# Decode value products in a hybrid decoder step: four pages per interruption of the weight products instead of two

## The chip, the cores and the metric

The kernel runs on one core of a Trainium2 chip. The metric is the device time of one execution in microseconds (us), as the median of several runs. TensorE does the matrix products, VectorE (DVE), ScalarE (ACT) and GpSimd (POOL) the rest; SyncE (SP) issues most of the DMAs.

## What is computed

One step of a decoder layer with two parallel groups, for a prompt of 512 tokens and for 8 sequences that each decode one token against 2048 cached positions (16 pages of 128 positions):

```
z = rms_norm(x) @ w_in                       # q | k | v | forget logits | lru x | lru gate
att: softmax(q.k/sqrt(d) + forget bias) @ v  # 8 heads of 128; decode rows read paged keys and values
lru: causal conv -> RG-LRU -> gelu(gate) * h # 8 blocks of 128 channels
x = x + concat(rms_norm(att), rms_norm(lru)) @ w_out
x = x + relu(rms_norm(x) @ w_up)^2 @ w_down
```

The change concerns the decode part of `softmax(...) @ v`: for each of the 8 sequences the probabilities of 2048 cached positions times the cached values, page by page. One value page is 128 positions x 8 heads x 128, 512 KB.

## The kernel before

The 520 token columns (512 of the prompt, 8 decoded) stay in on-chip memory, split into a high and a low part, `XH` and `XL`. The input weights come in units of 128 columns (1 MB each, two DMAs into `RAW`); ScalarE copies a unit into its high part `WH` (L743, `split_hi`), VectorE subtracts to get the low part `WL` (L1213, `split_lo`), and TensorE does 16 x 6 products of 128x260 per unit (L1896 and L1900). There are two slots of each buffer.

The middle of the kernel is eight steps, i = 0 to 7, one per attention head, per recurrent block and per decode sequence at once. A step has four units, q = 0 to 3, and TensorE's order in it is written out by hand: a unit has 32 half-steps n, and `insert` names what is done behind half-step n. "(q, n)" below is such a place. In step i stand:

- the value products of sequence i-1 (`VALUES_AT`) and the rest of those of sequence i-2 (`OLDER_AT`): eight interruptions of two pages each. They are the calls of TensorE's `values`, which multiply one column of probabilities (`PP`) by a page in `VR`, at L2057. Each page, once done, releases its slot (`v_used`);
- `queries` at (0,13), `max_rows` at (0,15), `max_all` at (0,25) (L2160), `head_scores` at (1,5) (L2084 to L2086), `transpose_probs` at (2,7) (L2095), `attend` at (2,19) (L2105), `rows` at (3,7), and the recurrent gates (L2247) at the end.

VectorE's order is written out too. Behind `max_all` it subtracts the maximum (`shift`, L1422 and L1423), finishes the recurrence, copies the query (`next_query`, L1499), scores key pages 0 to 3 (L1349 and L1351), splits a weight unit (L1213), takes the row maxima of the prompt's scores (L1506), scores pages 4 and 5, and scales the probabilities (`normalized`, L1517); `transpose_probs` waits for those. Then follow further key pages, the convolution (L1403 to L1408), a split, and the last key pages.

Value pages go through a ring of `NVS` = 4 slots in `VR`, key pages through another of 4 in `KR`. SyncE issues, in order, the value pages (L524) and the weight units (L439); before it asks for a page it waits until the page four earlier is used. GpSimd issues the key pages from a queue of its own. After step 7 come the output units (`out_unit`), in which the last pages of sequence 6 and all of sequence 7 are done, and then the feed-forward part.

Of the kernel before, what the change touches and what calls it, by code (L numbers as in the profile page):

```python
# [19 lines left out]
def hymba_step(nc, x_prompt, x_sample, cache_k, cache_v, cache_logf, state_conv, state_h, page_table,  # L20
# [14 lines left out]
    NB = x_sample.shape[0]  # L35
# [4 lines left out]
    NH, HD = cache_k.shape[3], cache_k.shape[4]  # L40
    DA = NH * HD
    NL = (D - DA) // P
    NPG = page_table.shape[1]
# [7 lines left out]
    NKS, NVS = 4, 4  # L51
# [45 lines left out]
    with ExitStack() as ctx:  # L97
# [214 lines left out]
        def at(n, half):  # L312

            return n % 2, n // 2 + half
# [11 lines left out]
        def one(i):  # L326
            return bass.ds(i, 1)
# [81 lines left out]
        PT_BANK = [(4, 0), (5, 0), (6, 0), (6, 256)]  # L409
        PT_AT = [0, 512, 896, 1152]  # L410

        VALUES_AT = {(1, 21): 0, (2, 5): 2, (2, 21): 4, (3, 5): 6, (3, 21): 8}
        OLDER_AT = {(0, 5): 10, (0, 21): 12, (1, 3): 14}
        MT_PS, MAX_PS = PS[0:NH, 6, P:2 * P], PS[:, 6, 2 * P:2 * P + NH]
        MT_LAST, MAX_LAST = PS[0:NH, 4, 3 * P:4 * P], PS[:, 5, 3 * P:3 * P + NH]
        VO = PS[:, 7, 0:2 * HD]
# [8 lines left out]
        def _(sp):  # L425
            def load_unit(n, half, src, peeled=False):
                slot, w = at(n, half)
                if not peeled:

                    sp.wait_ge(lo_done, 2 * w + slot - 1)  # L430
                for part in range(2):
                    load_part(slot, src, part)
# [8 lines left out]
            def cols(view, c):  # L441
                return view[:, :, bass.ds(c, P)]
# [6 lines left out]
            for j in range(TT):  # L449
                sp.dma_start(XT[:, j, :], x_prompt[0, j * P:(j + 1) * P, :]).then_inc(x_in[j], 16)  # L450
                for src, r in rows[3 * j:3 * j + 3]:
                    n = src.shape[0] * src.shape[1] // P
# [30 lines left out]
            def out_cols(u):  # L483

                rows = slice(NH, KD) if u < CH else slice(0, NH)
                c = P * out_tile(u % CH, 0)
                return w_out_v[:, rows, c:c + 2 * P]

            def step(i, head, prev, nxt, older=True):
                def values(h, pages):  # L490
                    for b in pages:
                        value_page(h, b, not older)

                for q in range(4):
                    if q == 0 and prev and older:
                        values(i - 2, range(12, 14))
                    if q and prev:
                        values(i - 1, range(4 * q - 4, 4 * q - 2))
                    if head:
                        src = [lambda: cols(w_in_v, COL_X + P * i), lambda: cols(w_in_v, COL_G + P * i),  # L500
                               lambda: cols(w_in_v, DA + P * (i + 1)) if nxt else out_cols(0),
                               lambda: cols(w_in_v, 2 * DA + P * (i + 1)) if nxt else out_cols(1)][q]()
                        load_unit(U_L + 2 + q, 2 * i, src)
                    else:
                        load_unit(U_O + 2 + q, 0, out_cols(2 + q))
                    if head and q == 1:
                        if prev:
                            sp.wait_ge(gates_ps, i)
                        sp.dma_start(GW[:, 0, :], w_gate_a[0, one(i), :, :].rearrange("a p c -> p (a c)")).then_inc(gw_full, 16)
                        sp.dma_start(GW[:, 1, :], w_gate_x[0, one(i), :, :].rearrange("a p c -> p (a c)")).then_inc(gw_full, 16)  # L510
                    if q == 0 and prev and older:
                        values(i - 2, range(14, NPG))
                    if q and prev:
                        values(i - 1, range(4 * q - 2, 4 * q))
                if not head:
                    load_unit(U_O + 6, 0, out_cols(6))
                    values(i - 1, range(12, NPG))

            def value_page(h, b, first):

                g = page(h, b)
                if not first or b >= NVS:
                    sp.wait_ge(v_used, NPG * h + b - NVS + 1)
                sp.dma_start(VR[:, b % NVS, :], v_pages[one(g), :, :].rearrange("a p f -> p (a f)"))\  # L524
                  .then_inc(v_full[b % NVS], 16)
# [1358 lines left out]
        def _(pe):  # L1884
# [51 lines left out]
            def out_unit(u, insert={}):  # L1936

                slot, w = at(U_O + u, 0)
                k0 = NH if u < CH else 0
                pe.wait_ge(lo_done, 2 * w + slot + 1)  # L1940
                for m in range(2):
                    out_products(u, m, range(k0, k0 + NH), {n - 2 * NH * m: f for n, f in insert.items()})
# [23 lines left out]
            for j in range(TT):  # L1966
                pe.wait_ge(x_in[j], 16)
                for c in range(4):
                    if j:
                        pe.wait_ge(x_ready[1], 4 * (j - 1) + c + 1)  # L1970
                    for n in range(4):
                        k = 4 * c + n
# [42 lines left out]
            for j in range(TT - 1):  # L2015
                n = TT - 1 - j
# [25 lines left out]

            unit(U_L - 1, 0, U_L - 1, 0, {17: [first_rows]})

            def values(h, b0):

                if b0 == 0:
                    pe.wait_ge(pp_ready, h + 1)
                    if isinstance(h, int) and h == 0:
                        pe.wait_ge(vo_clear, 1)  # L2050
                    else:
                        pe.wait_ge(pvs_ready, h)
                for b in (b0, b0 + 1):
                    pe.wait_ge(v_full[b % NVS], 16 * (NPG // NVS * h + b // NVS + 1))
                    for n in range(NH):
                        half, m = n // NHH, n % NHH
                        ins = mm(PS[VQ * m:VQ * m + 1, 7, half * HD:(half + 1) * HD], PP[:, n, b:b + 1],  # L2057
                                 VR[:, b % NVS, n * HD:(n + 1) * HD], start=b == 0 and half == 0, stop=b == NPG - 1,
                                 skip_group_check=True)
                    ins.then_inc(v_used, 1)  # L2060
# [28 lines left out]
            def transpose_probs(h):  # L2089

                pe.wait_ge(p_norm, h + 1)
                for j in range(TT):
                    bank, c = PT_BANK[j]
                    for t in range(j, TT):
                        ins = tr(PS[:, bank, c + (t - j) * P:c + (t - j + 1) * P],  # L2095
                                 PR[:, P_AT[t] + j * P:P_AT[t] + (j + 1) * P], ident[:, :])
                    if j != 2:
                        ins.then_inc(pt_ps, 1)

            def attend(h):  # L2100

                pe.wait_ge(vtok_ready, h + 1)
                for j in range(TT):
                    pe.wait_ge(pt_ready, 3 * h + min(j + 1, 3))
                    ins = mm(PS[:, 4, j * P:SEQ], vtok[:, j, :], PT[:, PT_AT[j]:PT_AT[j] + (TT - j) * P],  # L2105
                             start=j == 0, stop=j == TT - 1)
                ins.then_inc(att_ps, 1)
# [44 lines left out]
            def max_rows(i, dst=MT_PS):  # L2152

                pe.wait_ge(m8_ready, i)
                tr(dst, M8[:, :], ident[:, :]).then_inc(mt_ps, 1)

            def max_all(i, dst=MAX_PS):

                pe.wait_ge(md_ready, i)
                mm(dst, ones[0:NH, :], MD[:, :], start=True, stop=True).then_inc(max_ps, 1)  # L2160

            def step(i, head, prev, older=True, final=False):
# [54 lines left out]
                def places(q, n):  # L2217

                    f = []
                    if prev and (q, n) in VALUES_AT:  # L2220
                        f.append(lambda: values(i - 1, VALUES_AT[q, n]))
                    if prev and older and (q, n) in OLDER_AT:
                        f.append(lambda: values(i - 2, OLDER_AT[q, n]))
                    if (q, n) in extra:
                        f.append(extra[q, n])
                    return f
# [32 lines left out]
            h, last_b = NH - 1, NB - 1  # L2259
            slot, w = at(U_O, 0)  # L2260
            pe.wait_ge(lo_done, 2 * w + slot + 1)
            for k in range(NH, KD):
                for m in range(2):
                    out_products(0, m, [k], ready={0: (xl_ready, KD + k - NH + 1)})
                if k == NH + 1:
                    values(last_b - 1, 10)
                if k == NH + 4:
                    values(last_b - 1, 12)

            def head_scores():  # L2270
                pe.wait_ge(shifted, NB)
                scores(h, last=True)
                value_cols(last_b - 1)

            out_unit(1, {3: [lambda: values(last_b - 1, 14)], 7: [lambda: max_rows(NB, MT_LAST)], 11: [lambda: max_all(NB, MAX_LAST)],
                         14: [head_scores]})
            out_unit(2, {7: [lambda: transpose_probs(h)], 13: [lambda: values(last_b, 0)], 19: [lambda: attend(h)],
                         27: [lambda: values(last_b, 2)]})
            out_unit(3, {3: [lambda: values(last_b, 4)], 11: [lambda: values(last_b, 6)], 19: [lambda: values(last_b, 8)],
                         27: [lambda: values(last_b, 10)]})  # L2280
            out_unit(4, {3: [lambda: values(last_b, 12)], 11: [lambda: values(last_b, 14)], 17: [last_states], 23: [merge_sums]})
            out_unit(5, {5: [lambda: value_cols(last_b)], 13: [lru_sums]})
            out_unit(6, {3: [att_sums]})
            out_unit(7, {13: [sample_rows]})
# [188 lines left out]
```

## Time and profile before

| | |
|---|---|
| median of 3 runs | 2301.18 us (2300.08 to 2302.46) |
| span of the profiled execution | 2298.8 us |
| TensorE matmul busy | 2255.5 us, 98% |
| VectorE busy | 1605.5 us, 70% |
| ScalarE busy | 858.9 us, 37% |
| DMA over the span | 160 GB/s |
| value products (L2057) | 2048 records, 67.8 us busy |

The profile gives the busy time of each engine, groups of instructions by source line, who waited for whom, and the chain of work that ended last, followed back from the last instruction. Matmuls are pipelined, so the distance between two starts tells more than the length of one. A row of the timeline gives the start, the length of the run of like instructions, engine, line, operation, operands, how many, and in square brackets the idle time before it with what ended it. An fp32 product shows as two records.

### The profile page before, as it was taken

How to read it: one execution, taken by the hardware profiler on the slowest of the kernel's cores; microseconds unless marked ns; L12 is line 12 of the kernel's file. 1: busy time of each engine (PE TensorE's matmuls, PEld its weight loads, DVE VectorE, ACT ScalarE, POOL GpSimd, SP SyncE). 2: the span in 40 equal slices, each digit the busy share in tenths (PEclk: the TensorE clock that was granted, in tenths of full speed). 3: DMA queues.
4: the chain of work that ended last, by engine and by line, in shares of the span. 5: the costliest groups of instructions: out<-in, count | busy, mean ns of one | idle time of the engine just before them, and what ended most of it. 6: DMA issues, size and time to landing. Idle time of an engine off the chain costs nothing.

```text
span 2298.8 us, 50026 instructions
## 1 busy us (share of the span) xinstructions
PE 2255.5 (98%) x19889; PEld 2196.1 (96%) x19889; DVE 1605.5 (70%) x2043; ACT 858.9 (37%) x1201; POOL 154.0 (7%) x194
## 2 busy tenths in 40 slices
PE   7999999999999999999999999999999999999997
PEld 6999898989988999999999999999999999999997
DVE  7349889988884597876576576576576576576563
ACT  5124433344454233343243243243243243243245
POOL 0001111111114031000000000000000000000002
PEclk8999999999999999999999999999999999999998
DMA  7458999999985333333433433433433433433422
GB/s 239 106 159 261 323 330 327 317 314 327 317 290 191 98 127 84 114 96 99 138 93 98 137 93 98 137 93 99 137 94 98 137 93 99 137 93 99 137 89 97
DMA packets 386972, 368.47 MB, mean 160 GB/s; under 512 B 12259, under 2 KB 350596, under 8 KB 385844
## 3 DMA queue, kind: packets, MB, share of 16 engines
q1 hardware_dynamic: 359828, 295.38, 41.9%
q0 software_dynamic: 18608, 67.64, 8.2%
q10 hardware_dynamic: 8448, 4.20, 0.6%
q8 instruction: 65, 1.06, 0.2%
q14 instruction: 23, 0.19, 0.0%
HBM read 354.22 MB, written 12.94 MB: 160 GB/s over the span
## 4 chain that ended last, share of the span: by engine, by line
PE 87%; DVE 6%; DVEq 2%; issue 2%; ACT 1%; DMA 1%; SPq 1%; ACTq 0%
PE PS L1896 37%; PE PS L1900 18%; PE PS L2344 9%; PE PS L2343 9%; PE PS L2342 9%; DVE KR L1349 2%; PE PS L2057 2%; DVEq L1507 1%; PE PS L2105 1%; DVE WL L1213 1%; PE PS L2247 1%; DVE SC L1351 0%; ACT WH L743 0%; PE PS L2095 0%; DVE NM L1506 0%
## 5 line engine op out<-in xcount | busy, mean ns | idle before, releaser
L1093 ACT ACTIVATE WH<-RAW 128x1024 fp32r<-128x1024 f32 x293 | 304.9, 1056 | 679.8 <-PE PS L1900 521.5
L1647 DVE TENSOR_TENSOR WL<-RAW,WH 128x1024 fp32r<-128x1024 f32 x293 | 358.3, 1223 | 133.8 <-ACT WH L1093 132.4
L1896 PE MATMUL PS<-XH,WH 128*128 128x260 f32 x1952 | 408.6, 291 | 10.4 <-DVE XL L1278 6.2
L1896 PE MATMUL PS<-HH,WH 128*128 128x260 f32 x2048 | 412.5, 282 | 1.4 <-DVE HL L1652 0.7
L1900 PE MATMUL PS<-HH,WL 128*128 128x260 f32 x2048 | 411.7, 282 | 0.0
L1896 PE MATMUL PS<-HL,WH 128*128 128x260 f32 x2048 | 410.8, 282 | 0.0
L1896 PE MATMUL PS<-XL,WH 128*128 128x260 f32 x1952 | 393.7, 283 | 0.0
L1900 PE MATMUL PS<-XH,WL 128*128 128x260 f32 x1952 | 393.3, 283 | 0.0
L1750 DVE TENSOR_TENSOR A<-A,PS 128x520 f32<-128x520 f32 x256 | 177.5, 696 | 264.5 <-PE PS L1900 263.8
L1896 PEld LDWEIGHTS PS<-XH,WH 128*128 128x128 f32 x1952 | 301.4, 189 | 28.3 <-issue 19.5
L1896 PEld LDWEIGHTS PS<-HH,WH 128*128 128x128 f32 x2048 | 314.6, 188 | 2.1 <-issue 1.1
L1896 PEld LDWEIGHTS PS<-HL,WH 128*128 128x128 f32 x2048 | 316.1, 188 | 0.0
L1900 PEld LDWEIGHTS PS<-HH,WL 128*128 128x128 f32 x2048 | 315.4, 188 | 0.0
L1900 PEld LDWEIGHTS PS<-XH,WL 128*128 128x128 f32 x1952 | 302.3, 189 | 0.0
L1896 PEld LDWEIGHTS PS<-XL,WH 128*128 128x128 f32 x1952 | 302.1, 189 | 0.0
L2342 PE MATMUL PS<-XH,WH 128*128 128x260 f32 x960 | 271.6, 283 | 0.0
L2344 PE MATMUL PS<-XH,WL 128*128 128x260 f32 x960 | 271.0, 282 | 0.0
L2343 PE MATMUL PS<-XL,WH 128*128 128x260 f32 x960 | 270.9, 282 | 0.0
L1213 DVE TENSOR_TENSOR WL<-RAW,WH 128x2048 fp32r<-128x2048 f32 x61 | 139.6, 2288 | 105.2 <-ACT WH L743 105.1
L2343 PE MATMUL PS<-TX,WH 128*128 128x260 f32 x720 | 203.4, 283 | 0.0
L2344 PE MATMUL PS<-TX,WL 128*128 128x260 f32 x720 | 203.3, 282 | 0.0
L2342 PE MATMUL PS<-TX,WH 128*128 128x260 f32 x720 | 202.4, 281 | 0.0
(335 smaller groups left out, 3085.6 us busy)
## 6 DMA issues: line engine op xcount, KB each, us to landing
KR<-in_cache_k POOLq DMA_DIRECT2D x128, 512.0 KB, 6.0
VR<-in_cache_v SPq DMA_DIRECT2D x128, 512.0 KB, 6.3
RAW<-in_w_up SPq DMA_DIRECT2D x128, 512.0 KB, 4.2
RAW<-in_w_down SPq DMA_DIRECT2D x128, 512.0 KB, 4.5
RAW<-in_w_in SPq DMA_DIRECT2D x82, 512.0 KB, 6.6
RAW<-in_w_out SPq DMA_DIRECT2D x32, 512.0 KB, 5.5
TMP<-in_w_up SPq DMA_DIRECT2D x30, 512.0 KB, 6.1
xT_spill<-A SPq DMA_DIRECT2D x1, 4160.0 KB, 16.3
```

The lines of the kernel that those rows point to most:

```text
L1093: nc.scalar.activation(RING_H[SLOT[i]], RB[b], ACT.Copy).then_inc(f_hi, 1)
L1213: V.tensor_tensor(WL[slot][:, :], RAW[:, slot, :], WH[slot][:, :].bitcast(F32), ALU.subtract)\
L1349: V.tensor_tensor(KR[:, b % NKS, :], KR[:, b % NKS, :], QB[:, :], ALU.mult).then_inc(dve_prod, 1)
L1507: dve.drain()
L1647: V.tensor_tensor(RING_L[SLOT[i]], RB[op_block(i)], RING_H[SLOT[i]].bitcast(F32), ALU.subtract).then_inc(f_lo, 1)
L1750: V.tensor_tensor(rows, rows, pair_view(pair), ALU.add).then_inc(d_out[pair // 2], 1)
L1896: mm(dsts[c], wh(k), x[:, k, c * HT:(c + 1) * HT], start=first and n == 0 and x is xh, stop=False)
L1900: ins = mm(dsts[c], wl(k), xh[:, k, c * HT:(c + 1) * HT], start=False, stop=last and n == len(kts) - 1)
L2057: ins = mm(PS[VQ * m:VQ * m + 1, 7, half * HD:(half + 1) * HD], PP[:, n, b:b + 1], VR[:, b % NVS, n * HD:(n + 1) * HD], start=b == 0 and h ...
L2342: mm(dst, wh[:, w], xh[:, k, :], start=q < 3 and k == 0, stop=False, skip_group_check=True)
L2343: mm(dst, wh[:, w], xl[:, k, :], start=False, stop=False, skip_group_check=True)
L2344: ins = mm(dst, wl[:, w], xh[:, k, :], start=False, stop=q in (3, 5, 6) and k == KB - 1, skip_group_check=True)
```

## The change

The value products of a sequence are taken four pages at a time instead of two. In step i the places are now (1,21), (2,21) and (3,21) for pages 0 to 3, 4 to 7 and 8 to 11 of sequence i-1, and (0,21) for pages 12 to 15 of sequence i-2. The places (2,5), (3,5), (0,5) and (1,3) are no longer used. SyncE asks for the four pages of a unit ahead of the unit's weights, where it asked for two ahead of them and two behind. In output unit 0 the call for pages 10 and 11 of sequence 6 is dropped, since they are now done in step 7; the calls behind it, all of sequence 7 among them, keep their two pages.

```diff
-        VALUES_AT = {(1, 21): 0, (2, 5): 2, (2, 21): 4, (3, 5): 6, (3, 21): 8}
-        OLDER_AT = {(0, 5): 10, (0, 21): 12, (1, 3): 14}
+        VALUES_AT = {(1, 21): 0, (2, 21): 4, (3, 21): 8}
+        OLDER_AT = {(0, 21): 12}
...
+                ahead = 4 if head else 2
                 for q in range(4):
                     if q == 0 and prev and older:
-                        values(i - 2, range(12, 14))
+                        values(i - 2, range(12, 12 + ahead))
                     if q and prev:
-                        values(i - 1, range(4 * q - 4, 4 * q - 2))
+                        values(i - 1, range(4 * q - 4, 4 * q - 4 + ahead))
...
                     if q == 0 and prev and older:
-                        values(i - 2, range(14, NPG))
+                        values(i - 2, range(12 + ahead, NPG))
                     if q and prev:
-                        values(i - 1, range(4 * q - 2, 4 * q))
+                        values(i - 1, range(4 * q - 4 + ahead, 4 * q))
...
-            def values(h, b0):
+            def values(h, b0, pages):
...
-                for b in (b0, b0 + 1):
+                for b in range(b0, b0 + pages):
...
-                        f.append(lambda: values(i - 1, VALUES_AT[q, n]))
+                        f.append(lambda: values(i - 1, VALUES_AT[q, n], NVS))
                     if prev and older and (q, n) in OLDER_AT:
-                        f.append(lambda: values(i - 2, OLDER_AT[q, n]))
+                        f.append(lambda: values(i - 2, OLDER_AT[q, n], NVS))
...
-                if k == NH + 1:
-                    values(last_b - 1, 10)
                 if k == NH + 4:
-                    values(last_b - 1, 12)
+                    values(last_b - 1, 12, 2)
```

## Rows read from the trace of the kernel before

**Rows 1.** The page: span, and busy time of TensorE's matmuls and weight loads

```profile
span 2298.8 us, 50026 instructions
...
PE 2255.5 (98%) x19889; PEld 2196.1 (96%) x19889; DVE 1605.5 (70%) x2043; ACT 858.9 (37%) x1201; POOL 154.0 (7%) x194
```

**Rows 2.** Windows: one head step, busy us of each engine, granted clock, DMA share

```profile
core 0: us, PE busy (x) PEld busy (x) DVE busy (x) ACT busy (x) POOL busy (x), PEclk, DMA share, GB/s
...
477.90:545.10 67.20, 66.76 (x702) 60.53 (x701) 60.48 (x78) 26.98 (x44) 8.45 (x16) 1.00 0.95 322
```

**Rows 3.** TensorE's timeline round one interruption, and all value products by line

```profile
499.24 0.40 PE L1900 MATMUL PS<-XH,WL 128*128 128x260 f32 x2
499.57 1.05 PE L2057 MATMUL PS<-VR,PP 128*1 128x128 f32 x32
500.56 0.51 PE L1896 MATMUL PS<-XH,WH 128*128 128x260 f32 x2
500.90 0.41 PE L1896 MATMUL PS<-XL,WH 128*128 128x260 f32 x2
...
L2057 PE MATMUL PS<-VR,PP 128*1 128x128 f32 x2048 | 67.8, 272 | 2.2 <-DMA VR<-in_cache_v 2.2
```

**Rows 4.** The chain that ended last, same step: start us, us, what

```profile
478.20 0.61 DVEq L1375
...
488.97 1.22 DVE KR L1349
...
500.66 1.29 DVE PR L1517 x4
501.99 1.31 PE PS L2095 x10
...
510.49 0.98 PE PS L2057 x32
```

**Rows 5.** TensorE's timeline, same step, only the inserted work

```profile
483.12 0.38 PE L2084 MATMUL PS<-kT,qcur 128*128 128x128 f32 x2
...
501.99 1.20 PE L2095 MATMUL PS<-ident_r,PR 128*128 128x128 f32 x9 [0.44 <-DVE PR L1517]
...
510.42 1.05 PE L2057 MATMUL PS<-VR,PP 128*1 128x128 f32 x32
...
525.16 1.05 PE L2057 MATMUL PS<-VR,PP 128*1 128x128 f32 x32
...
529.84 1.88 PE L2247 MATMUL PS<-XC,GW 128*128 128x512 f32 x4
```

**Rows 6.** VectorE's timeline, same step

```profile
477.84 0.17 DVE L1422 COPY MX<-PS 128x8 f32 x1 [1.27 <-PE PS L2160]
...
481.48 0.41 DVE L1499 COPY qcur<-A 128x512 f32 x1
...
500.66 1.27 DVE L1517 TENSOR_SCALAR PR<-PR,RSUM 128x128 f32<-128x128 f32 x4
...
527.73 0.19 DVE L1408 COPY CVALL<-XW 128x24 f32 x1
```

**Rows 7.** TensorE's waits, 196 to 760 us: total us, times, longest

```profile
PE PS L2095 <- DVE PR L1517: 3.8, 6, 1.6
...
PE PS L2155 <- DVE M L1493: 1.6, 1, 1.6
```

**Rows 8.** The chain that ended last, from step 7's gates on

```profile
665.69 0.36 PE PS L2249 x4
...
667.65 1.81 ACT WH L743
...
687.26 0.30 DVE M L1493
687.60 0.29 PE PS L2155
```

**Rows 9.** SyncE's page requests; page landings in 511:525 (step 5), 242:257, 578:592

```profile
511.24 1.50 SPq L524 DMA_DIRECT2D VR<-in_cache_v  x2
...
DMA to landing us min/median/max: 5.0/7.5/9.2
...
DMA to landing us min/median/max: 5.5/9.8/12.6
...
DMA to landing us min/median/max: 7.3/10.0/13.7
```

**Rows 10.** Weight requests in 580:586 with their landings, and the split that reads them

```profile
L439 SPq DMA_DIRECT2D RAW<-in_w_in x2: 384/467/550, 581.0 to 581.6; - x2
...
DMA to landing us min/median/max: 7.8/11.4/15.0
...
600.75 1.93 ACT L743 ACTIVATE WH<-RAW 128x2048 fp32r<-128x2048 f32 x1
```

More of the change, by code:

```diff
@@ L2273, in head_scores @@
                 value_cols(last_b - 1)
-            out_unit(1, {3: [lambda: values(last_b - 1, 14)], 7: [lambda: max_rows(NB, MT_LAST)], 11: [lambda: max_all(NB, MAX_LAST)],
+            out_unit(1, {3: [lambda: values(last_b - 1, 14, 2)], 7: [lambda: max_rows(NB, MT_LAST)], 11: [lambda: max_all(NB, MAX_LAST)],
                          14: [head_scores]})
[L2277 to L2281, printed above, removed]
+            out_unit(2, {7: [lambda: transpose_probs(h)], 13: [lambda: values(last_b, 0, 2)], 19: [lambda: attend(h)],
+                         27: [lambda: values(last_b, 2, 2)]})
+            out_unit(3, {3: [lambda: values(last_b, 4, 2)], 11: [lambda: values(last_b, 6, 2)], 19: [lambda: values(last_b, 8, 2)],
+                         27: [lambda: values(last_b, 10, 2)]})
+            out_unit(4, {3: [lambda: values(last_b, 12, 2)], 11: [lambda: values(last_b, 14, 2)], 17: [last_states], 23: [merge_sums]})
             out_unit(5, {5: [lambda: value_cols(last_b)], 13: [lru_sums]})
```

## The prediction

> **What bounds the kernel now.** I read first the profile's first part, then the windows of one head step, then the chain that ended last. TensorE is busy 98% of the span [rows 1], so the change, which takes work from TensorE, looks like pure gain. The windows warn: in a head step (67.2 us) TensorE is busy 66.76 us, VectorE 60.48 us and the DMA engines 0.95 of the time [rows 2]. Three resources are nearly full, and which ends last must be read place by place. The clock is granted in full there (1.00 in the same row, the 2.4 GHz level), so no term here changes with it.
>
> The chain of waits answers it [rows 4]. In each head step it leaves TensorE when the cross-head maximum is done (`max_all`, half-step (0,25)), runs through VectorE alone, and comes back to TensorE at `transpose_probs`, half-step (2,7), where TensorE had stood idle 0.44 us for the scaled probabilities [rows 5]. VectorE begins that stretch having waited 1.27 us for TensorE, at 477.84, and ends it at 501.93 (500.66 + 1.27): 24.1 us in which it waits for nothing of note [rows 6]. From (2,7) round to the next (0,25) the chain is TensorE's own. So one period is the sum of two parts: 24.1 us of VectorE plus the handovers, then TensorE from (2,7) to (0,25). TensorE's work from (0,25) to (2,7) is no part of the sum; it is 0.44 us shorter than VectorE's.
>
> **What an interruption costs.** The value products of two pages are 32 records in 1.05 us [rows 3]. They run four at a time: eight fours, each record 0.27 us long, so a four follows the last after (1.05 − 0.27)/7 = 0.11 us, and a page, four fours, is 0.44 us. The weight products start a pair every 0.24 us. Round an interruption the starts go 499.24, then 500.56 and 500.90; undisturbed the last of them would be at 499.72. The interruption therefore takes 1.18 us, of which 0.88 is pages and 0.30 is switching in and out. A page costs the same wherever it stands; only the 0.30 can be saved.
>
> **What the change removes.** All value products are 2048 records, so 64 interruptions of 32 [rows 3]. After the change heads 0 to 5 take four each (24), head 6 takes three of four pages and two of two (5), head 7 keeps its eight: 37. Gone are 27, worth 27 × 0.30 = 8.1 us of TensorE's time. No trace row shows a group of 64 records. From one side, its second half could cost nothing extra; from the other, it could run slower than 0.11 us per four. The nearest row is the uniform group of 32, so I take 0.44 us a page, with no surcharge.
>
> **Where the work lands.** Now the two parts separately.
> - (0,25) to (2,7): the groups at (1,3) and (2,5) go, the one at (1,21) doubles. TensorE saves 2 × 1.18 − 0.88 = 1.48 us here. VectorE's 24.1 us are untouched (the change doesn't edit it, and its start hangs on (0,25)), so TensorE arrives earlier and waits longer: 0.44 + 1.48 = 1.92 us at `transpose_probs`. Worth to the period: nothing. At (1,5) `head_scores` loses its 1.23 us of slack as well (VectorE's query copy ends at 481.89, TensorE comes at 483.12 [rows 5, 6]); a tenth of a us of wait there would be inside the same cover.
> - (2,7) to (0,25): the groups at (3,5) and (0,5) go, those at (2,21), (3,21) and (0,21) double. Before: 5 groups with 10 pages. After: 3 groups with 12 pages, because pages 14 and 15 came across from (1,3). That is 2 × 0.44 − 2 × 0.30 = +0.28 us, on the path, each step.
>
> So a change that saves TensorE time makes the period longer. Six such sections lie between the (2,7) of steps 1 to 6 and the (0,25) of steps 2 to 7: +1.7 us. The cover exists in each: the wait at `transpose_probs` is there in steps 1 to 6, six times, 3.8 us in all, 1.6 us the longest (step 1, which only gets longer) [rows 7]; step 7 has a wait near zero, so there at most 0.05 us is gained.
>
> The last step: from its (2,7) to its gate products the groups at (2,21) and (3,21) double and (3,5) goes, 0.88 − 0.30 = +0.58 us. From the gates the chain is ScalarE's and VectorE's up to `max_rows` [rows 8], where TensorE stands idle 1.6 us [rows 7]. The removed group of pages 10 and 11 in output unit 0 is under that idle time: it becomes 1.6 + 1.18 us of waiting, and the end is 0.58 us later. Behind that nothing is changed; head 7 keeps its pairs, and its waits for pages hang on TensorE's own release of slots.
>
> The wait of VectorE for `max_all` covers small slips: from the gates to (0,25) TensorE gets 1.18 − 0.88 = 0.30 us shorter, leaving 1.27 − 0.30 = 0.97 us.
>
> **What SyncE's queue does.** Its four requests are made at the same point as its first two were: each waits for the slot of four pages earlier, free only when the products at the (q,21) before are done. Two requests take 1.50 us from the first's start to the second's end, so they follow each other at about 1.17 us. The fourth is out about 0.83 + 3 × 1.17 = 4.3 us after the group starts at 510.42 [rows 5, 9]. Queued behind them are the unit's two weight requests, moved back by 2 × 1.17 = 2.3 us and behind 1 MB more, and at q = 1 the gate weights. ScalarE's split waits for these weights. In the slowest case a weight part took 15.0 us to land (asked 581.6, landed 596.6) and the split began at 600.75 [rows 10]: 4.1 us of slack, which 1 MB at 320 GB/s [rows 2] cuts by 3.3 us. With the 0.97 us above I take zero here; its upper bound is a few tenths of a us in one step. Key requests are in GpSimd's queue and are not moved; VectorE's page scores behind (2,7) have 2 us of cover up to the gate products (convolution done at 527.92, gates at 529.84 [rows 5, 6]), plus the new 0.58.
>
> **Sum.** 6 × 0.28 + 0.58 = 2.3 us. The profiled span is 2298.8 us, the median of the runs 2301.18, so 2.4 us lie around the span. I forecast a span of 2301.1 and a time of 2303.4 us: +0.10%, no change that a measurement of this kernel tells from zero (it takes about 0.2%, 4.6 us: 2296.6 to 2305.8). The 0.30 is the softest number: with 0.42 the sum is 1.2 us, with 0.20 it is 3.6, so 2302.4 to 2304.8.
>
> **Rivals.**
> 1. The saving counts in full. If VectorE's stretch were no bound, because it could start its part earlier or has slack that the chain doesn't show, all 8.1 us would go: 2293.1 us. For it speaks TensorE's 98%; against it the chain of rows 4 and the same wait in six steps. The Trainium skill's "Perfetto Trace Analysis" (section Identifying the Most-Contended Engine) says to optimize the engine of highest occupancy first, though it distrusts matmul busy time as a measure; by its first half this rival's time is the forecast, and rows 4 speak against it. Chance 0.10, the case between included.
> 2. Pages late at (3,21), the other side. The shortest of the intervals between groups is (2,21) to (3,21), 14.74 us, now 0.30 shorter, and the fourth page is read 3 × 0.44 us into the group: it must be there 15.8 us after the group before it began. It is asked for at 4.3, so a landing over 11.5 us stalls TensorE on the path, one for one. Landings in this stretch: 5.0 to 9.2 us in a usual step, up to 12.6 in step 1 and 13.7 in step 6 [rows 9]. Were the fourth page the slow one in both, the stalls are 1.1 and 2.2 us: 2303.4 + 3.3 = 2306.7 us, slower by 0.24%. Against it: those slow ones stood behind the weights in SyncE's queue, and now the pages go first. The Trainium skill's "DMA: Bandwidth & Descriptors" (section Queues, rings and completion order) has each DMA engine take its queues in turn, packet by packet; by that rule four pages asked for at once share with the key pages of the other queue and the fourth lands late, which is this mechanism. Chance 0.16.
> 3. The doubled group runs slower than two single ones (an issue limit that 32 records don't reach). Three doubled groups are in each on-path section; a second half at double time adds 3 × 0.88 × 6 = 16 us: 2319. Chance 0.04.
> 4. The forecast, 0.70.
>
> **Range and chances.** 2299.5 to 2307.5 us: the upper end takes in rival 2, the lower one a part of rival 1; left out are the full gain and rival 3. Faster 0.10, same 0.70, slower 0.20.
>
> **What would show it.** In the changed trace: 37 groups, those of four pages about 1.9 us long with 2.06 us from last to next regular start; the wait at `transpose_probs` about 1.9 us in steps 2 to 7 and in step 1 as well; VectorE's stretch still 24.1 us; the period about 67.4 us; TensorE's wait at `max_rows` about 2.8 us. If the wait at `transpose_probs` stays near 0.44 and the period falls to 66, step one of the reading is wrong; if idle time before (3,21) goes to pages, rival 2 is right.

## The result, and the profile after

| | before | after |
|---|---|---|
| median | 2300.64 us (20 runs) | 2304.07 us (20 runs) |
| lowest to highest | 2298.89 to 2302.46 | 2302.14 to 2305.78 |
| span of the profiled execution | 2298.8 us | 2303.9 us |

The ratio is 1.0014, with a 95% interval of 1.0008 to 1.0021. The change makes the kernel 3.4 us slower. The forecast was 2303.4 us, 2.3 us above the 2301.18 us that three runs of before had given; over 20 runs before is at 2300.64. TensorE is less busy than before and the kernel takes longer:

```profile
span 2303.9 us, 50021 instructions
...
PE 2252.2 (98%) x19889; PEld 2202.1 (96%) x19889; DVE 1605.5 (70%) x2043; ACT 858.1 (37%) x1201; POOL 154.6 (7%) x194
```

**The group of four pages.** TensorE's timeline round one of them (start, length, engine, line; the lines are one further on than before):

```profile
494.33 0.40 PE L1901 MATMUL PS<-XH,WL 128*128 128x260 f32 x2
494.66 1.93 PE L2058 MATMUL PS<-VR,PP 128*1 128x128 f32 x64
496.51 0.51 PE L1897 MATMUL PS<-XH,WH 128*128 128x260 f32 x2
496.86 0.41 PE L1897 MATMUL PS<-XL,WH 128*128 128x260 f32 x2
```

From 494.33 to 496.86 are 2.53 us, less 0.48 for two undisturbed pairs: 2.05 us, where two groups of two took 2 x 1.18 = 2.36 [rows 3]. One switch saves 0.31 us, and 64 records in a row run as fast as 32.

**Where the step's time went.** The window of one step, TensorE's timeline at `transpose_probs` in it, and VectorE's at its first and last operation of the stretch:

```profile
480.80:548.30 67.50, 65.76 (x701) 60.83 (x701) 60.45 (x76) 26.86 (x44) 8.47 (x16) 1.00 0.96 320
```

```profile
505.01 1.31 PE L2096 MATMUL PS<-ident_r,PR 128*128 128x128 f32 x10 [1.74 <-DVE PR L1518]
```

```profile
480.86 0.17 DVE L1423 COPY MX<-PS 128x8 f32 x1 [0.98 <-PE PS L2161]
...
503.68 1.27 DVE L1518 TENSOR_SCALAR PR<-PR,RSUM 128x128 f32<-128x128 f32 x4
```

TensorE's busy time in the step fell from 66.76 to 65.76 us [rows 2], and its wait rose from 0.44 to 1.74 us [rows 5]. VectorE's stretch is 503.68 + 1.27 - 480.86 = 24.09 us, as before [rows 6]. From one `transpose_probs` to the next the traces give 67.18 us before and 67.46 us after, +0.28 each. The chain that ended last shows why: it passes from VectorE to TensorE at `transpose_probs`, and the doubled groups at (2,21), (3,21) and (0,21) are on it; the one at (1,21) is not.

```profile
503.68 1.28 DVE PR L1518 x4
505.01 1.31 PE PS L2096 x10
...
513.51 1.86 PE PS L2058 x64
...
527.95 1.86 PE PS L2058 x64
...
544.27 1.86 PE PS L2058 x64
...
548.68 0.61 DVEq L1376
```

**What the forecast didn't have.** In step 1 TensorE waited 1.84 us at the same place, and right behind it its granted clock stood at half for 3.4 us, the 1.2 GHz level. TensorE's timeline, and the window of that stretch (the granted clock is the number ahead of the DMA share; the same window of before has 1.00, with 31 matmuls in it where here are 16):

```profile
233.54 2.30 PE L2096 MATMUL PS<-ident_r,PR 128*128 128x128 f32 x10 [1.84 <-DVE PR L1518]
235.49 0.78 PE L1897 MATMUL PS<-XH,WH 128*128 128x260 f32 x2
```

```profile
233.50:236.90 3.40, 3.36 (x16) 3.36 (x17) 3.37 (x3) 2.11 (x7) 0.17 (x1) 0.53 1.11 349
```

The ten transposes took 2.30 us here and 1.31 us in each of steps 2 to 7. The next `transpose_probs` came 69.07 us later instead of 67.46: the fall cost 1.6 us.

The trace has a second fall of the same length. It begins behind a wait of 2.12 us in output unit 0, where TensorE waits for the low part of a recurrent block:

```profile
683.63 0.50 PE L1897 MATMUL PS<-XH,WH 128*128 128x260 f32 x2 [2.12 <-DVE XL L1242]
...
691.76 0.27 PE L2156 MATMUL PS<-ident_r,M 128*8 128x128 f32 x1 [0.80 <-DVE M L1494]
```

```profile
684.20:687.60 3.40, 3.40 (x18) 3.37 (x17) 3.37 (x5) 2.06 (x3) 0.00 (x0) 0.51 0.19 60
```

This one cost nothing. The slower products used up part of the time in which TensorE would have waited for VectorE at `max_rows`: that wait is 0.80 us here where before had 1.6 [rows 7]. In the trace of run 5 below, which has the same wait of 2.12 us and no fall behind it, the way from there to `max_rows` is 8.12 us, and here 8.13.

**The ledger of the two traces.** Start-up to step 1: +0.3. Step 1 to 2: +1.9, of which 0.28 is the step and 1.6 the clock. Steps 2 to 7: 5 x 0.28 = +1.4. Step 7 to `max_rows`: +0.58. Head 7's page waits: +0.9, TensorE's worst one being 1.85 us where 0.90 stood. The sum is 5.1 us, the difference of the spans. The medians differ by 3.4. With one trace of each kernel it is not shown in how many executions the fall or the longer page wait occurs. The granted clock of the whole span is known for every run, and its mean is 0.9930 over the 20 runs of the changed kernel, against 0.9943 over the 15 runs of before that stood beside runs 5 to 8, and 0.9946 over the 11 runs of run 5. That speaks for falls in many runs, but a start-up with more time at half clock would lower it as well.

### The profile page after: what moved, and what is told of

Read it like the earlier page. It is cut to its first block, busy times and chain, and to the rows that moved or that the text cites. A ratio compares the mean times of both kernels' runs of the same rounds, so it can differ in the third digit from the quotient of the medians.

```text
span 2303.9 us, 50021 instructions
## 1 busy us (share of the span) xinstructions
PE 2252.2 (98%) x19889; PEld 2202.1 (96%) x19889; DVE 1605.5 (70%) x2043; ACT 858.1 (37%) x1201; POOL 154.6 (7%) x194
## 4 chain that ended last, share of the span: by engine, by line
PE 86%; DVE 7%; DVEq 2%; issue 2%; ACT 1%; DMA 1%; ACTq 0%; SPq 0%
PE PS L1897 36%; PE PS L1901 18%; PE PS L2343 9%; PE PS L2342 9%; PE PS L2341 9%; DVE KR L1350 2%; PE PS L2058 2%; DVEq L1508 1%; DVE SC L1352 1%; PE PS L2106 1%; DVE WL L1214 1%; PE PS L2248 1%; PE PS L2096 0%; ACT WH L744 0%; DVE NM L1507 0%
```

## The experiments

Each was run beside the kernel before on its chip; "before" in the text is that kernel's median there. Diffs are cut to the lines that matter.

A caution for all traces below: the way from the start to step 1's `transpose_probs` differs by more than a microsecond from trace to trace. It is 233.3 us before and 233.5 after the change, but 232.0 and 232.1 in runs 4 and 5. The granted clock differs too, in a start-up in which all kernels run the same code: from 28.5 to 35 us it is 0.52 before and 0.50 after the change, and 1.00 in runs 4 and 5. The window before, and that of run 4:

```profile
28.50:35.00 6.50, 4.96 (x22) 4.76 (x23) 6.35 (x10) 3.19 (x5) 0.00 (x0) 0.52 1.10 451
```

```profile
28.50:35.00 6.50, 4.23 (x33) 4.02 (x34) 6.33 (x10) 3.27 (x6) 0.00 (x0) 1.00 1.08 443
```

So the traces are compared stretch by stretch, and not by their spans.

**1. Shorten VectorE's stretch in the changed kernel.**

```diff
                 if head:
-                    score(i, range(4, 6))
+                    score(i, range(4, 5 if prev else 6))
                 if prev:
                     denominators(h)
...
                 if head:
-                    score(i, range(6, 8))
+                    score(i, range(5 if prev else 6, 8))
```

> The changed kernel, with one edit in VectorE's order: key page 5 is scored behind the scaling of the probabilities instead of ahead of it, which takes 2.43 us out of VectorE's stretch from the maximum to transpose_probs. Theory A (the period is VectorE's stretch plus TensorE's work from (2,7) to (0,25), and the switches saved elsewhere only became waiting): TensorE's waits at transpose_probs, 1.84 + 5 x 1.74 + 1.49 = 12.0 us in the changed kernel, go to nearly nothing, and the time falls to about 2292 us. Rival B (the saved switches went into something else, late pages or weights, and VectorE's stretch is no bound): 2304 us as the changed kernel, within 1 us.

Measured: 2294.85 us, before 2301.06 (ratio 0.9972, 0.9961 to 0.9983). One of the eight executions took 6552 us; the median of the other seven is 2294.31 us, and that is used from here on. 9.8 us came off the changed kernel by moving 2.43 us of VectorE's work to the other side of one TensorE wait. Some of it is the clock: with the long waits, both falls of the changed kernel's trace are gone, of which one had cost 1.6 us. Rival B is out. It missed the expected 2292 by 2.3 us: the waits at `transpose_probs` are all gone, but a new one stands at `queries`, where TensorE waits for a small copy that VectorE does behind the last key pages. TensorE's waits in the head steps of this run (us in total, times, longest):

```profile
PE PS L2180 <- DVE SELQ L1434: 2.3, 5, 0.6
```

**2. The same edit in the kernel before.**

> The kernel before, with the same edit in VectorE's order. Theory A: only the waits at transpose_probs that it had go, 1.56 + 5 x 0.44 = 3.8 us: about 2297 us, some 5 us above the same edit in the changed kernel, since TensorE's work is then on the path everywhere and the changed kernel has less of it. Rival B: no change, 2300.6 us.

Measured: 2298.52 us, before 2301.06 (0.9988, 0.9979 to 0.9997). -2.5 us, of 3.8 expected; TensorE's trace has three new waits of 0.24 to 0.67 us for weights, as VectorE now splits them 2.4 us later. It is 4.2 us above run 1, where some 5 were expected. The order of the two is as theory A wants it: the same edit is worth 9.8 us with four pages and 2.5 us with two, because the four-page kernel had more waiting to give back.

**3. Merge only on the path.**

```diff
-        VALUES_AT = {(1, 21): 0, (2, 5): 2, (2, 21): 4, (3, 5): 6, (3, 21): 8}
-        OLDER_AT = {(0, 5): 10, (0, 21): 12, (1, 3): 14}
+        VALUES_AT = {(1, 21): (0, 2), (2, 5): (2, 2), (2, 21): (4, 4), (3, 21): (8, 4)}
+        OLDER_AT = {(0, 21): (12, 2), (1, 3): (14, 2)}
```

(SyncE asks for pages 8 to 11 ahead of the weights; all other requests stand as before. The call in output unit 0 is dropped as in the change.)

> The kernel before, with groups merged only from (2,7) to (0,25): pages 4 to 7 at (2,21), 8 to 11 at (3,21); 12 and 13 stay at (0,21), 14 and 15 at (1,3), 0 and 1 at (1,21), 2 and 3 at (2,5). Theory A: two switches less on the path in each of six periods, no page moved onto it, -0.60 x 6, and +0.58 us in the last step: -3.0 us, 2297.6 us; the wait at transpose_probs stays 0.44 us. By the count of switches alone (14 gone, 0.30 each) -4.2 us. If merging itself costs something that the sums leave out (late pages, slower long groups), it is not faster than before.

Measured: 2297.52 us, before 2301.06 (0.9989, 0.9980 to 0.9998). Expected 2297.6. So close a hit is in part luck: six runs lie at 2296.5 to 2297.5 us and five at 2298.8 to 2300.4, and the interval allows a gain of 0.5 to 4.6 us. The trace is firmer: a step is 66.6 us where it was 67.18, the 0.60 us of two switches. The window of one step and the wait in it:

```profile
475.50:542.10 66.60, 66.16 (x701) 60.64 (x700) 60.45 (x77) 26.98 (x44) 8.45 (x16) 1.00 0.96 325
```

```profile
499.64 1.31 PE L2095 MATMUL PS<-ident_r,PR 128*128 128x128 f32 x10 [0.44 <-DVE PR L1517]
```

About half as many switches go as in the change, 14 against 27, and it gains what the change loses, because no page is moved out from under VectorE's stretch. TensorE has 0.4 us more work per step here than in the changed kernel, and the step is 0.9 us shorter.

**4. Merge only off the path.**

```diff
-        VALUES_AT = {(1, 21): 0, (2, 5): 2, (2, 21): 4, (3, 5): 6, (3, 21): 8}
-        OLDER_AT = {(0, 5): 10, (0, 21): 12, (1, 3): 14}
+        VALUES_AT = {(1, 21): (0, 4), (2, 21): (4, 2), (3, 5): (6, 2), (3, 21): (8, 2)}
+        OLDER_AT = {(0, 5): (10, 2), (0, 21): (12, 2), (1, 3): (14, 2)}
```

> The kernel before, with one merge that lies under VectorE's stretch: pages 0 to 3 at (1,21), nothing at (2,5), all else as before. Theory A: the wait at transpose_probs grows by the 0.30 us of the switch, to 0.74 us (1.86 us in step 1), and the time doesn't move: 2300.6 us. By the count of switches (7 gone) 2298.5 us. Theory C on the clock (in the changed kernel's trace TensorE's granted clock fell to half for 3.4 us right after the 1.84 us wait of step 1): if that longer wait is the cause, the same fall shows here in step 1 and adds some 1.6 us.

Measured: 2300.30 us, before 2301.06 (1.0001, 0.9992 to 1.0010): no change. The saved switch stands in the trace as waiting, 0.30 us more than before, and step 1's wait is 1.85 us:

```profile
502.25 0.98 PE L2095 MATMUL PS<-ident_r,PR 128*128 128x128 f32 x7 [0.74 <-DVE PR L1517]
```

Behind step 1's wait the granted clock fell here too, and nowhere else in the head steps:

```profile
233.00:236.40 3.40, 3.40 (x19) 3.40 (x17) 3.33 (x4) 3.40 (x7) 0.44 (x1) 0.52 1.02 407
```

From step 2's `transpose_probs` to step 6's the trace gives 268.70 us, before 268.72: the saved switches are worth nothing there, as theory A says. Step 1 to step 2 took 68.69 us instead of 67.18, so the fall cost 1.5 us. That the traced run is no longer than before in spite of it (spans of 2298.6 and 2298.8 us) comes from its start-up, 1.2 us shorter, and from 0.5 us less waiting for a page of head 7. So the median that didn't move is no evidence against a cost of the fall. Three of the eleven runs, at 2303.7 to 2304.6 us, stand apart from the other eight at 2299.7 to 2301.2; no trace of them was kept, and what they have is open.

**5. Take the long wait of step 1 away.**

```diff
-                ahead = 4 if head else 2
...
+                    ahead = 4 if head and (older or q != 2) else 2
...
+                        pair = not older and (q, n) == (1, 21)
+                        f.append(lambda: values(i - 1, VALUES_AT[q, n], 2 if pair else NVS))
+                    if prev and not older and (q, n) == (2, 5):
+                        f.append(lambda: values(i - 1, 2, 2))
```

> The changed kernel, with pairs kept in step 1 alone: pages 0 and 1 at (1,21), 2 and 3 at (2,5). Theory A on the path: nothing, since this lies under VectorE's stretch; step 1's wait at transpose_probs goes from 1.84 back to 1.54 us. Theory C on the clock (a wait of some 1.85 us in step 1 lets TensorE's granted clock fall to half for 3.4 us in part of the runs, at some 1.6 us): the fall at 234 us is gone from the trace, the upper half of the changed kernel's runs (2305 to 2306) is gone too, and the median comes down from 2304.1 to about 2302.8. If the fall has nothing to do with this wait, it stays and so does the median.

Measured: 2302.80 us (2301.78 to 2304.56), before 2300.97 (1.0008, 0.9999 to 1.0018). It went as theory C said: step 1's wait is 1.56 us, the trace has no fall of the clock between start-up and the end, the five runs of 20 above 2305 us have no like here, and the median is 1.3 us lower. The medians alone don't settle that 1.3, since the two were not run side by side: against its own before each is 3.4 us slower (1.8 to 4.8) and 1.8 us slower (-0.2 to 4.1). The traces do: the way from step 1's `transpose_probs` to step 2's is 67.46 us here and 69.07 in the changed kernel.

This trace is also the cleanest test of the forecast's sum, as no fall is mixed in. From step 1's `transpose_probs` to step 7's it gives 404.35 us, before 402.68: +1.67, where 6 x 0.28 = 1.7 was forecast. From there to `max_rows` it gives 52.22 us, before 51.65: +0.57, where 0.58 was.

**6. SyncE's order of before, with groups of four.**

```diff
-                ahead = 4 if head else 2
+                ahead = 2
```

> The changed kernel with SyncE's order of before: two pages, the unit's weights, two pages. TensorE's groups stay at four pages. Theory A: pages 10 and 11 land some 3 us later than in the changed kernel, where the last had 2.4 to 4.5 us to spare, so at most one or two steps wait, a us or less each: 2304 to 2306 us. Rival (the weights asked for later are what costs the changed kernel its time): faster than 2304, towards 2301.

Measured: 2346.04 us, before 2300.97 (1.017, 1.0144 to 1.0195); of the five runs three are at 2346.0 to 2347.8 us and two at 2332.8 and 2333.5. It is the largest effect of the study, and none of the theories expected it. TensorE's waits for pages in the head steps:

```profile
PE PS L2058 <- DMA VR<-in_cache_v: 31.0, 14, 6.0
```

SyncE's timeline in step 4 (start, length of the run of requests):

```profile
465.79 1.50 SPq L525 DMA_DIRECT2D VR<-in_cache_v  x2
468.39 1.18 SPq L439 DMA_DIRECT2D RAW<-in_w_in  x2
470.41 3.27 SPq L525 DMA_DIRECT2D VR<-in_cache_v  x1
```

The request for the third page, behind two weight requests, takes SyncE 3.27 us where one takes 0.33, so the fourth goes out only at 474.5, 8.7 us behind the first. That page landed at 483.3, and the group needed it at 481. In steps 1 to 6 the request of page 10, behind the weights in this way, took 2.9 to 4.4 us, and such pages also took longer to land: in step 2 the third and fourth landed 14.3 and 11.1 us after the start of their requests, where in the changed kernel the fourth took 7.4. In the changed kernel all four requests are out in 3.85 us, and the weights behind them bear the delay (step 5):

```profile
514.26 3.85 SPq L525 DMA_DIRECT2D VR<-in_cache_v  x4
518.39 3.12 SPq L439 DMA_DIRECT2D RAW<-in_w_in  x2
```

The waits are 31 us of the 42. In the head steps this trace has seven falls of the granted clock, 3.4 us (three) or 6.8 us (four) long, one in each step, at or behind the page waits. They are the likely place of the rest. At 1.6 us for each 3.4 us, the price from the changed kernel's step 1, step 1 to step 2 should take 67.46 + 5.49 of page waits + 3.2 = 76.15 us and step 4 to step 5 67.46 + 2.27 + 1.6 = 71.33; the trace has 75.94 and 71.60. For steps 2 and 3 the same estimate is within 0.4 us, for steps 5 and 6, where the fall begins during or before the waits, it is 1.1 and 1.4 us too high. No run took the falls away by themselves.

**7. Lengthen the wait.**

```diff
-                V.reciprocal(RSUM[:, :], SUMS[:, :])
-                dve.drain()
+                for _ in range(4):
+                    V.reciprocal(RSUM[:, :], SUMS[:, :])
+                    dve.drain()
```

> The changed kernel, with VectorE's reciprocal ahead of the scaling done four times instead of once (same result): its stretch grows by 3 x 0.24 = 0.72 us, the wait at transpose_probs to 2.5 us. Theory A: VectorE's stretch is on the path in each of steps 1 to 7, and once more behind step 7, so +0.72 x 7 or 8 = 5.0 to 5.8 us: 2309 to 2310 us. Theory B (the stretch is no bound): nothing. Theory C: if waits of over 1.8 us bring the clock down, falls show behind the waits of several steps, not of step 1 alone, and each adds up to 1.6 us on top.

Measured: 2309.05 us, before 2300.97 (1.0037, 1.0023 to 1.0050): 5.0 us over the changed kernel. From one `transpose_probs` to the next it is 68.21 us where the changed kernel has 67.46, +0.75 for 0.72 us of added work: the stretch is on the path one for one. On the clock theory C got only half: the waits are 2.48 us in steps 2 to 6, longer than any of the changed kernel, and the clock fell behind step 1's 2.61 us alone. Two windows of this run, step 1 and the same place of step 2:

```profile
233.00:236.40 3.40, 3.40 (x18) 3.40 (x19) 3.33 (x4) 2.39 (x7) 0.00 (x0) 0.52 1.08 355
303.00:306.40 3.40, 3.40 (x32) 3.40 (x30) 3.33 (x4) 3.02 (x7) 0.00 (x0) 1.00 1.08 359
```

The length of the wait doesn't decide by itself.

**8. Clear the next wait too.**

```diff
                 if head and not final:
+                    V.tensor_copy(SELQ[:, :], SEL[:, :, i + 1] if isinstance(i, int) else
+                                  SEL[:, :, one(i + 1)].rearrange("p n a -> p (n a)")).then_inc(qcol_ready, 1)
                     last_scores(i)
```

(with the edit of run 1, in the changed kernel; the copy is taken out of its old place)

> The changed kernel with key page 5 scored behind the scaling, as before (2294.9 us), and VectorE's copy of the query columns moved ahead of the last two key pages of a step. In that run's trace TensorE waits 0.35 to 0.62 us at queries, (0,13), in five steps, for this copy. Theory A: these waits go or move to max_rows at (0,15), 0.7 us further on: 2293 to 2294.5 us.

Measured: 2290.25 us (2288.80 to 2291.09), before 2300.97 (0.9952, 0.9938 to 0.9965). It is the fastest kernel of the study, 10.7 us ahead of before and 13.8 ahead of the change as it stood, and better than the 2293 to 2294.5 expected. Between steps 1 and 7 its trace is 4.2 us shorter than run 1's. 2.3 of them are the waits at `queries`, about half a microsecond is a wait at the gates of step 6 (0.26 us where run 1 had 0.73), and where the rest comes from was not followed up. One step of it:

```profile
472.10:537.60 65.50, 65.50 (x701) 60.78 (x700) 60.46 (x76) 26.87 (x44) 8.46 (x16) 1.00 0.97 330
```

TensorE is busy the whole step and waits for nothing that the trace shows, and DMA moves 330 GB/s. The wait didn't move to `max_rows`, as was allowed for.

**9. Both edits with two pages.**

```diff
                 if head:
-                    score(i, range(4, 6))
+                    score(i, range(4, 5 if prev else 6))
...
                 if head and not final:
+                    V.tensor_copy(SELQ[:, :], SEL[:, :, i + 1] if isinstance(i, int) else
+                                  SEL[:, :, one(i + 1)].rearrange("p n a -> p (n a)")).then_inc(qcol_ready, 1)
                     last_scores(i)
```

(in the kernel before, as in run 8)

> The kernel before with both edits of VectorE's order that the changed kernel had in the last run (key page 5 behind the scaling, the query columns copied ahead of the last two key pages); value pages in pairs at the eight places. Theory A: with no wait left at transpose_probs all eight places are on the path, so against the 2290.2 us of the changed kernel with both edits the four switches of each of six steps count in full, 6 x 1.24 = 7.4 us: about 2297 to 2298 us. That is, the merge that costs 3.4 us in the kernel as it was is worth 7 us here. If the switches had no worth of their own, the two would be equal.

Measured: 2297.32 us (2296.60 to 2299.16), before 2301.14 (0.9984, 0.9975 to 0.9993). The difference to run 8 is 7.1 us, expected 7.4. So the same merge costs 3.4 us in the kernel as it was and is worth some 7 us once VectorE's stretch doesn't bound. That all of it is switches is not shown: between steps 1 and 7 this trace is 8.8 us longer than run 8's, of which 1.8 us are three waits for weights (0.73, 0.67 and 0.44 us) that run 8 doesn't have, and its way to step 1 is 1.4 us shorter.

## Why the prediction was right, point by point

- **The price of a switch.** 0.30 us forecast, 0.31 measured, in a group that no trace row of before showed. Rival 3 (long groups run slower) is out.
- **The two parts of the period.** +0.28 us a step forecast and measured. Run 5's trace, which has no fall of the clock, gives +1.67 and +0.57 us for the two terms of the sum. Runs 3 and 4 take the two parts singly (-3.5 and -0.8 us of their own before's median, the second within its interval), run 7 lengthens VectorE's part and runs 1 and 2 shorten it; all go with the theory, and rival 1 is out. The wait at `transpose_probs` came to 1.74, not 1.92: a tenth is spent at `head_scores`, where TensorE now starts 0.15 us behind VectorE's query copy, and that was named; the other tenth was not traced.
- **The last step.** +0.58 forecast and measured. But the removed group's time didn't become waiting at `max_rows`. It went into an earlier wait in output unit 0, for the low part of the last recurrent block, which was not among the rows: 2.12 us where 0.93 stood, in the changed kernel's trace and in run 5's alike. The 2.8 us that the forecast named as a sign at `max_rows` didn't come: run 5 keeps 1.6, and the changed kernel has 0.80, because its second fall of the clock made TensorE come later. The sum was right with the wrong place.
- **Rival 2, late pages.** It didn't occur: no page wait in steps 1 to 7, and the fourth page of (3,21) had 2.4 to 4.5 us to spare. The landings of the four pages in steps 1 and 6 were at most 7.4 and 6.9 us, against 12.6 and 13.7 before [rows 9]. The argument put against it was that the slow ones had stood behind the weights, and the landings agree with it. Run 6 shows how much hung on the order of requests: with the old one there were page waits in each step. No wait for weights appeared in steps 1 to 7 either, as the zero in the forecast had it.
- **What was missing.** The forecast held the clock at 1.00 because before showed 1.00, and didn't ask what a longer idle time would do to it. It named the wait of step 1 as one that "only gets longer", at no cost; it cost 1.6 us in the trace, and the median is 1.3 us lower in run 5, which shortened the wait. The term wasn't in the sum. The trace also has 0.9 us more of page waits in head 7, but nothing ties these to the change: in the other ten traces the longest of them is 0.65 to 1.54 us, and the 1.54 is of run 9, which has pairs everywhere.
- **How much of the hit is luck.** The forecast added 2.3 us to 2301.18, the median of three runs; over 20 runs before is 0.5 us lower. The change was 3.4 us, 1.1 more than the sum, so the two misses partly cancel in 2303.4 against 2304.07. The forecast also said that so small a change couldn't be told from zero; with 20 runs of each it could (1.0008 to 1.0021).
- **A slip.** For a switch of 0.42 us the sum, by its own formula with 0.44 us a page, is 6 x 0.04 + 0.46 = 0.7 us and not 1.2, and the low end 2301.9 and not 2302.4. Nothing else hangs on it.
- **The clock's cause** is half settled. Shown: 1.84 to 2.61 us of waiting in step 1 came with a fall right behind it in the traces of the change, of run 4 and of run 7, about 1.56 us had none in three traces (before, run 3, run 5), and in run 5's trace, where the longer wait was taken away, the fall was gone. Each is one trace. Open: why waits of 1.7 to 2.5 us in steps 2 to 7 bring none, why 2.12 us in output unit 0 brought one in the changed kernel and none in runs 5 and 7, and why the trace of run 6 has 1.85 us in step 1 and its first fall only at the page wait after it.

## What to carry to other kernels

Before work is taken from the busiest engine, split its period at the places where it waits, and count only what goes between the wait and the next handover; the rest becomes a longer wait. Moving work out of a covered part into an uncovered one can cost more than the saving brings, and the gain is then had by shortening the covering engine's stretch: here 2.4 us of VectorE work behind one signal instead of ahead of it turned +3.4 us into -6.7, and with one more small copy moved into -10.7. Where traces are compared, compare the same stretch in both: a start-up that differs by 1.2 us hid a loss of 1.5 us in run 4. When a consumer takes several buffers at once, ask for them all ahead of anything large in the same queue.

## What the runs showed of the hardware

- A page request behind two weight requests, in a busy stretch, held SyncE for 3.27 us instead of 0.33 us (run 6). The Trainium skill's "DMA: Bandwidth & Descriptors" (section Issuing engines are not separate DMA queues) calls the issuing sequencer's time usually small relative to the transfer. The requests of 0.33 us agree; the one of 3.27 us, whose page landed 10.2 us after its start, doesn't. The order of requests was worth 42 us in this kernel; how that divides between requests made late and pages landing late was not taken apart.
- TensorE's granted clock went to the 1.2 GHz level for 3.4 us right behind single waits of 1.84 us (the change), 1.85 us (run 4) and 2.61 us (run 7) in stretches in which TensorE was otherwise busy. On the path each cost 1.5 to 1.6 us. A fourth, behind 2.12 us, cost nothing, as TensorE had to wait for VectorE behind it anyway. Five waits of 2.48 us in run 7 brought no fall.
- The same start-up code ran at different clocks in different runs: from 28.5 to 35 us the granted clock was 0.52 before the change and 1.00 in runs 4, 5 and 7.
